# Expert stage of a decoder layer: output copy moved behind silu, up grains ahead of it, the 32 certain steps written out

## What is computed

```
def expert_block(args):
    xblk, e = args
    return (jax.nn.silu(xblk @ w_gate[e]) * (xblk @ w_up[e])) @ w_down[e]
```

## Time and profile before

| | us |
|---|---|
| median of three runs | 3566.56 |
| lowest, highest | 3563.41, 3567.97 |
| the profiled execution, its own time | 3570.77 |
| its span, first to last instruction | 3568.9 |

### The profile page before, as it was taken

The page is one execution under the profiler, slowest core; times in us unless marked ns, Lnnn a source line. Parts: engine busy times, 40 slices in busy tenths (PEclk is TensorE's granted clock), DMA queues, the critical chain, the costliest instruction groups (busy, mean ns, idle before and its releaser), DMA issues. The chain is left out here.

```text
span 3568.9 us, 76160 instructions
## 1 busy us (share of the span) xinstructions
PE 3111.6 (87%) x27464; PEld 2515.2 (70%) x27464; DVE 2019.4 (57%) x2950; ACT 1596.5 (45%) x2656; POOL 879.0 (25%) x1064
## 2 busy tenths in 40 slices
PE   7999999988898848888888599569899999996899
PEld 5776878865666637777778488457777777774687
DVE  4333761017777724444444233668788788885555
ACT  3332211007777723333333111057777777775332
POOL 1001320002141366766674100000000000000343
PEclk9999999999999969999999799679999999998899
DMA  5444357444000031211110466536877866773343
GB/s 166 171 171 156 127 179 251 142 132 107 7 16 7 12 125 44 80 63 62 62 62 15 138 215 214 200 110 244 316 284 262 338 258 248 294 264 138 127 147 118
DMA packets 230272, 541.77 MB, mean 152 GB/s; under 512 B 26208, under 2 KB 62176, under 8 KB 221824
## 3 DMA queue, kind: packets, MB, share of 16 engines
q1 hardware_dynamic: 211696, 471.48, 37.5%
q0 software_dynamic: 11552, 41.95, 3.2%
q10 hardware_dynamic: 6768, 24.64, 1.7%
HBM read 408.52 MB, written 129.51 MB: 151 GB/s over the span
## 5 line engine op out<-in xcount | busy, mean ns | idle before, releaser
L559 PE MATMUL p_z<-w_in_part,hn_split 128*128 128x512 f32 x2304 | 538.7, 394 | 8.7 <-DVE w_in_part L388 4.5
L559 PEld LDWEIGHTS p_z<-w_in_part,hn_split 128*128 128x128 f32 x2304 | 435.3, 190 | 100.1 <-DMA hn_split<-s_hT 5.0
L1670 DVE TENSOR_TENSOR e_w_part<-w_gate_up_sb,e_w_part 128x1024 fp32r<-128x1024 f32 x380 | 441.1, 1220 | 105.2 <-ACT e_w_part L1665 105.2
L1665 ACT CAST e_w_part<-w_gate_up_sb 128x1024 fp32r x380 | 372.3, 1046 | 134.0 <-PE pe_y L2420 71.0
L2408 PE MATMUL pe_gate<-e_w_part,e_xT 128*128 128x512 f32 x1128 | 288.6, 414 | 32.8 <-DVE e_w_part L1670 32.8
L2408 PE MATMUL pe_up<-e_w_part,e_xT 128*128 128x512 f32 x1128 | 274.8, 399 | 16.7 <-DVE e_w_part L1670 16.6
L2420 PE MATMUL pe_y<-e_w_part,e_hT 128*128 128x512 f32 x1128 | 277.2, 402 | 7.3 <-DVE e_w_part L1670 7.3
L2408 PEld LDWEIGHTS pe_gate<-e_w_part,e_xT 128*128 128x128 f32 x1128 | 219.1, 198 | 84.7 <-DVE e_w_part L1670 24.4
L2408 PEld LDWEIGHTS pe_up<-e_w_part,e_xT 128*128 128x128 f32 x1128 | 208.8, 188 | 81.2 <-DVE e_w_part L1670 33.1
L2420 PEld LDWEIGHTS pe_y<-e_w_part,e_hT 128*128 128x128 f32 x1128 | 210.4, 190 | 55.1 <-DVE e_w_part L1670 7.7
L1670 DVE TENSOR_TENSOR e_w_part<-w_down_sb,e_w_part 128x1024 fp32r<-128x1024 f32 x188 | 223.5, 1222 | 21.7 <-ACT e_w_part L1665 19.1
(11 more groups left out here) (422 smaller groups left out, 5946.9 us busy)
## 6 DMA issues: line engine op xcount, KB each, us to landing
w_gate_up_sb<-in_w_gate_dram SPq DMA_DIRECT2D x32, 2048.0 KB, 15.1
w_gate_up_sb<-in_w_up_dram SPq DMA_DIRECT2D x32, 2048.0 KB, 19.8
w_down_sb<-in_w_down_dram SPq DMA_DIRECT2D x32, 2048.0 KB, 9.8
hn_split<-s_hT SPq DMA_DIRECT2D x48, 1024.0 KB, 5.1
s_y<-e_y ACTq DMA_DIRECT2D x47, 512.0 KB, 7.2
s_hT<-hn_split SPq DMA_DIRECT2D x16, 1024.0 KB, 6.5
s_y<-d_zeros SPq DMA_DIRECT2D x16, 1024.0 KB, 6.6
s_zr<-z_stage SPq DMA_DIRECT2D x48, 256.0 KB, 2.0
```

Of the source, the lines that this page charges most:

```text
L559: last = nc.tensor.matmul(bank, hs[m % 3][:, a, k, :].bitcast(F32R), w_part(c, b)[:, k, :].bitcast(F32R), start=(k == 0 and a == b == 0), ...
L1665: return nc.scalar.copy(high, src)
L1670: return nc.vector.tensor_tensor(low, src, high, ALU.subtract)
```

## The change

On ScalarE the output copy and its store go from the end of step i-1 (then for block i-2, ahead of hT) to behind silu of step i, for the same block i-2. `copy_hT` is written at the end of the step before on ScalarE and VectorE. The up grains of a written-out step use the slot number that `gate` had read. Steps 0 to 31 are written out; the tail stores two blocks, and for that the table of ends has one more entry.

```diff
         def steps(eng, body, tail):

             last = eng.value_load(ends[0:1, EXPERTS - 1:EXPERTS], min_val=BLOCKS // 2 + 1, max_val=BLOCKS)
-            for i in range(4):
+            for i in range(BLOCKS // 2):
                 body(i)
-            with eng.Fori(2, BLOCKS // 4) as j:
-                for s in range(2):
-                    body(j * 2 + s)
             with eng.Fori(BLOCKS // 4, BLOCKS // 2) as j:
...
         @block.scalar
...
             def gate(i):

                 loaded(i, gu_in, 1)
-                slot = act.value_load(tab[0:1, 0, bass.ds(i, 1)], min_val=0, max_val=SLOTS - 1)
+                slots[known(i)] = slot = act.value_load(tab[0:1, 0, bass.ds(i, 1)], min_val=0, max_val=SLOTS - 1)
...
             def up(i):

-                slot = act.value_load(tab[0:1, 0, bass.ds(i, 1)], min_val=0, max_val=SLOTS - 1)
+                slot = slots[known(i)] if known(i) is not None else act.value_load(tab[0:1, 0, bass.ds(i, 1)], min_val=0, max_val=SLOTS - 1)
...
             def body(i):
-                if known(i) != 0:
-                    copy_hT(i - 1)
                 up(i)
                 act.wait_ge(gu_used, i * 8 + 4)
                 if known(i) != 0:
                     act.wait_ge(h_done, i)
                 nc.scalar.activation(sg[:], p_g[:], ACT.Silu).then_inc(silu_done, 1)
+                if known(i) is None or i >= 2:
+                    store_y(i - 2)
                 if known(i) != 0:
                     down(i - 1, lambda g: act.wait_ge(gu_used, i * 8 + (5 + g)))
                 copy_xT(i + 1)
                 gate(i + 1)
-                if known(i) != 0:
-                    store_y(i - 1)
+                copy_hT(i)

             def tail(i):
-                copy_hT(i)
+                store_y(act.value_load(ends[0:1, 3 * EXPERTS + 1:], min_val=BLOCKS // 2 - 2, max_val=BLOCKS - 3))
                 down(i, lambda g: act.wait_ge(gu_low, i * 8 + (g + 10)))
                 store_y(i)
...
         @block.vector
...
             def gate_up(i, first):

-                slot = dve.value_load(tab[0:1, 0, bass.ds(i, 1)], min_val=0, max_val=SLOTS - 1)
+                if known(i) is None or first == 0:
+                    slots[known(i)] = dve.value_load(tab[0:1, 0, bass.ds(i, 1)], min_val=0, max_val=SLOTS - 1)
+                slot = slots[known(i)]
...
             def body(i):
-                if known(i) != 0:
-                    copy_hT(i - 1)
                 gate_up(i, 4)
...
                 copy_xT(i + 1)
                 gate_up(i + 1, 0)
+                copy_hT(i)

             def tail(i):
-                copy_hT(i)
                 down(i)
```

More of the change, by code:

```diff
@@ L2114, in _ @@
             v.tensor_scalar(ends[0:1, E:2 * E], ends[0:1, 0:E], 8, 7, ALU.mult, ALU.subtract)
-            v.tensor_scalar(ends[0:1, 3 * E:], ends[0:1, E - 1:E], 2, None, ALU.subtract)
+            for k in range(2):
+                v.tensor_scalar(ends[0:1, 3 * E + k:3 * E + k + 1], ends[0:1, E - 1:E], 2 + k, None, ALU.subtract)
             v.tensor_scalar(ends[0:1, 2 * E:3 * E], ends[0:1, 0:E], 4, 3, ALU.mult, ALU.subtract)
@@ L2223, in steps @@
                         body(j * 2 + s)
-            tail(eng.value_load(ends[0:1, 3 * EXPERTS:], min_val=BLOCKS // 2 - 1, max_val=BLOCKS - 2))
+            tail(eng.value_load(ends[0:1, 3 * EXPERTS:3 * EXPERTS + 1], min_val=BLOCKS // 2 - 1, max_val=BLOCKS - 2))
         @block.gpsimd
@@ L2267, in loaded @@
                     act.sem_inc(passed_act, 1)
+            slots = {}
             def gate(i):
                 loaded(i, gu_in, 1)
-                slot = act.value_load(tab[0:1, 0, bass.ds(i, 1)], min_val=0, max_val=SLOTS - 1)
+                slots[known(i)] = slot = act.value_load(tab[0:1, 0, bass.ds(i, 1)], min_val=0, max_val=SLOTS - 1)
                 for g in range(4):
@@ L2706, in block_kernel @@
         wts = sb("expert_weights", [P, TILES, 2]); dest = sb("expert_rows", [P, 2, TILES], U32)
-        ids = sb("row_tokens", [P, BLOCKS + 1], U32); tab = sb("block_table", [1, 2 + SLOTS + DOWN_SLOTS, BLOCKS + 2], I32); ends = sb("turn_ends", [1, 3 * EXPERTS + 1], I32)
+        ids = sb("row_tokens", [P, BLOCKS + 1], U32); tab = sb("block_table", [1, 2 + SLOTS + DOWN_SLOTS, BLOCKS + 2], I32); ends = sb("turn_ends", [1, 3 * EXPERTS + 2], I32)
         order = sb("turn_experts", [1, EXPERTS], I32)
```

## The result

The changed kernel takes 3623.4 us (median of four runs, 3617.73 to 3627.97), the kernel before 3566.62; the ratio is 1.0156, with a 95% interval from 1.0144 to 1.0169. The profiled execution has a span of 3626.2 against 3568.9, so 57.3 us more. The forecast was slower, 3627.

What follows compares the result with a forecast made beforehand. TensorE, busy 87% of the span, was taken as the bound. Terms +27.4 (22 steps), +8.1 (weight waits), +17.7 (loop), +7.5 (tail) gave +60.7: 3631.5 on the profiled execution, 3627 us against the median, range 3594 to 3660.

Steps and rivals of the forecast that it cites:

- The step that decides: ScalarE behind silu: store holds back three table loads, first down cast at T + 10.7, new TensorE wait of 1.2 us.
- second wait: TensorE before the next gate: VectorE, running late, delays the first gate grain, 0.25 us a step.
- The 22 steps: Written-out steps without a weight wait: 19.8 us each in place of 18.78, in all +27.4 us.
- two slow gates: Two gates at half clock just after weight waits, among the 22 steps: + 5 us.
- the loads pass the store: Faster rival: ScalarE's sequencer goes on past the waiting store, first down cast at T + 8.4; 3551 us, chance 0.12.
- Slow loads: Three ScalarE table loads behind the store, some slower than the 278 ns median: 0.3 us a step, bounds 0 to 1.2.
- the slow rival: Two of the three loads behind each store take 889 ns, 0.9 us more in 44 steps: 3667 us, chance 0.06.
- The eight steps with weight waits: Two groups of four: weight loads issued later, waits do not shrink; +1.35 and +2.7 us, twice, +8.1.
- The loop: Steps 32 to 45, still looped: ten at 20.2 us add 13.7, two pairs 2 each, +17.7 us.
- the two pairs: Looped step pairs that hold a weight wait, among steps 32 to 45: 2 us more each.
- Tail: Last block's hT is copied before the 17 skipped steps, so its first down cast comes later: +7.5 us.
- Writing out alone: Writing the steps out without reordering: 22 steps at 18.1 us in place of 413.2 in all, 15 us saved.

Runs made afterwards that it cites:

- e3: Changed kernel with the three down-weight table loads moved ahead of the output copy and its store: 3569.23 us, ratio 1.0001 to the kernel before.
- e5: Changed kernel with the output copy left behind silu and only the store's issue moved behind the four down casts: 3562.71 us, ratio 0.9984.
- e4: Changed kernel with hT's copy back at the start of the step and in the tail, on ScalarE and VectorE: 3622.16 us, ratio 1.0148.
- e1: Kernel before with steps 0 to 31 written out and nothing else, ScalarE's order the old one: 3563.22 us against 3568.95, ratio 0.9987.
- e7: Changed kernel with the down slot read twice, one more table load between store and down casts: 3671.29 us, ratio 1.0291.

## Why the prediction was right, point by point

- **The step that decides** was what stands behind the store in ScalarE's order, and it held: no wait at pe_up, 44 waits at pe_y, the loads start after the store. First down cast, predicted T + 10.7 before slow loads and 11.0 with them, 10.81 in step 16 and 11.2 at the median; second wait 0.25, as the steps without a weight wait show (hT to gate 0.60 in place of 0.35).
- **The 22 steps** at 19.8 and two slow gates made 440.6; measured 440.81. That they meet to 0.2 is luck, two errors that cancel: only one gate ran at the lower clock, in step 12, for 2.3 us and not 5 (steps 24 to 31 have a granted clock of 1.00), and the other 21 steps take 19.93 and not 19.8, by the slow loads.
- **The rival "the loads pass the store"** is out by the order in which they start, and e3 and e5 show what it would have given, with the loads put ahead of the issue by hand: 3569 and 3563, not 3551. Its price was too good: it takes 4 us off the eight steps with weight waits and 3 off the two pairs, but the waits for weights grew, to 25.3 and 24.2 us. Its comparison, that the sequencer goes on past the waits of casts as of silu, holds for silu alone: in step 3 of the kernel before the table loads start at T + 6.06, only when the last up cast's wait for its ring place, which stands in register work of the sequencer (FUSED_REGOPS, done at T + 5.92), is met.
- **Slow loads**: 0.3 a step was low. Second and third add 0.27 and 0.19, 0.46 on average, and two at 889 ns in every step, the slow rival, was far too much. Slowness goes with the place behind the store and not with the line. The floor of some 600 ns that the prediction cites from the Trainium skill's "DMA: Bandwidth & Descriptors" is not seen: ScalarE's undisturbed loads stay under 0.3 us.
- **The eight steps with weight waits**: +5.4 for +8.1. w_down's load in step 8 is issued at T + 17.22 for the 16.9 of the sum, so its starting point held. The first group, +4.8, is near its term of 4.05; the second gave +0.6, as its two waits for weights fell from 3.5 and 4.4 us to 3.1 and 0.2. The term that failed is that these waits do not shrink. In e4, whose steps have the same order, the wait ahead of step 24 is 4.1 us, so its absence here is a matter of one execution.
- **The loop**: 17.8 for 17.7, but by two errors. The ten steps cost 16.6 (292.21 - 84.83 = 207.4) and not 13.7, as slow loads were under-priced (0.53 a step there for 0.3); the two pairs +1.2 and not +4, as their weight waits did shrink, from 2.8 and 4.3 us to 1.2 and 2.2.
- **Tail**: +9.8 for +7.5 (the prediction's own sum, 3279.8 less 3272.05, gives 7.7). The mechanism is as predicted; the wait at pe_y of the last step was 1.8 where the tail's sum has 0.5, though the step's own sum has 1.2 and the slow loads; and running through the skipped steps took 8.15 for 7.6 (3316.83 to 3324.98).
- **Writing out alone** was put at 15 us for the 22 steps; e1 shows 10.8. The 15 leaves out the half clock of two gates, for which the prediction's sum for the loads that pass the store has 5 us more and comes to 10.

The mechanism is shown; the terms miss by up to 3 us each and in both directions, so that the total, 60.6 inside the stage and behind it for a predicted 60.7, is closer than the working deserves. 57.3 is what the profiles differ by, 56.8 the medians.

What stays open is why table loads, on either engine, are slow behind a store. That the store reads the same memory then is a guess; no run changed its size or its source.

## What to carry to other kernels

Before the issue of a transfer that waits is moved on a queue, list what follows it in the order of issue, register loads included: work that ran ahead under a long operation is on the path as soon as a blocking issue stands in front of it, and neither its engine's busy time nor the name in the wait list shows it. Copy and issue can be placed apart, the copy where its buffer must come free and the issue behind the last urgent cast, but not so late that its landing holds the next copy. When steps wait for loads in some places, price a gain in the others against the time at which those loads are issued.

## What the runs showed of the hardware

- A semaphore wait on a transfer's issue stopped ScalarE's sequencer: in step 16 of the changed kernel the issue starts 0.03 us behind the end of its copy and the first table load 0.03 us behind the issue. Silu does not stop it: in step 3 of the kernel before silu starts at T + 6.91, and the loads run from T + 6.06 to 7.58. "Advanced Engine Details and Errata" in the Trainium skill (Sequencer Loop) says that other engine instructions can be read and queued while a control instruction executes; it does not say there whether an issue that waits is one. This trace does not show it for such an issue: what stands behind it came after it, and moving the loads ahead removed some 55 us.
- ScalarE's table load takes 0.272 to 0.293 us undisturbed (the gate slot's in the changed kernel). From 0.4 to 3 us behind the issue of a 512 KB store from ScalarE's queue many take 0.5 to 1.2 us, and on VectorE, 0.30 to 0.32 undisturbed, 24 of 44 in e5 did.
- TensorE's clock fell to 1.2 GHz not only behind the 4 to 5 us waits for weights but in e7 also behind single waits of 2.0 to 3.0 us at pe_y, at full speed before, in 18 of 44 steps; behind waits as long the down matmuls of the other 26 kept 2.4 GHz (5.8 us). In the changed kernel waits of 1.0 to 2.0 us in nearly every step mostly left it at 2.4 GHz (PEclk 1.00 in steps 24 to 31).
